# Reordering the head of a two-layer decoder trunk: row factor, head rotations, first weight load and last means

## What is computed

```
for layer in range(2):
    h = rms_norm(x, ln1_g)                  # x * rsqrt(mean(x*x) + eps) * g
    P = h @ w_in                            # 2124 columns: heads of three groups
    a = dsa_mixer(...)                      # indexer scores, top 64 keys, 4 heads, partial rotary
    b = s5_mixer(...)                       # complex diagonal state space, 16 groups of 16
    c = nsa_mixer(...)                      # compressed, selected and window branches, 8 heads
    x = x + concat(rms_norm(a), rms_norm(b), rms_norm(c)) @ w_out
    x = x + square(relu(rms_norm(x, ln2_g) @ w_up)) @ w_down
return rms_norm(x, final_g)
```

## Time and profile before

| | |
|---|---|
| time before, median of 3 runs | 732.26 us (732.01 to 736.17) |
| the profiled execution's own time | 735.1 us |
| its span | 733.1 us |
| PE busy | 664.8 us, 91% |
| DVE busy | 450.8 us, 61% |
| ACT busy | 367.1 us, 50% |
| POOL busy | 228.2 us, 31% |
| mean granted TensorE clock | 0.967 |

### The profile page before, as it was taken

The page is one execution under the profiler, slowest core; times in us unless marked ns, Lnnn a source line. Parts: engine busy times, 40 slices in busy tenths (PEclk is TensorE's granted clock), DMA queues, the critical chain, the costliest instruction groups (busy, mean ns, idle before and its releaser), DMA issues.

```text
span 733.1 us, 11482 instructions
## 1 busy us (share of the span) xinstructions
PE 664.8 (91%) x4308; PEld 586.9 (80%) x4308; DVE 450.8 (61%) x860; ACT 367.1 (50%) x680; POOL 228.2 (31%) x379
## 2 busy tenths in 40 slices
PE   5959878779899999999999987977989999999996
PEld 4847767568798899988978886756879889999884
DVE  8675974843755559596555659584375555455553
ACT  5542755563544543445545567556354444444542
POOL 5899433441034399980000001544100000000001
PEclk9988998998999999999999999999899999999998
DMA  9485020200685555637535722020065665666541
GB/s 267 125 220 149 30 41 30 73 30 29 202 237 201 170 186 169 225 119 247 168 119 164 228 79 41 30 73 30 29 202 178 196 188 171 208 182 198 177 140 57
DMA packets 62965, 102.77 MB, mean 140 GB/s; under 512 B 20677, under 2 KB 27022, under 8 KB 62878
## 3 DMA queue, kind: packets, MB, share of 16 engines
q1 hardware_dynamic: 58862, 98.63, 44.1%
q0 software_dynamic: 592, 1.70, 0.9%
q10 hardware_dynamic: 3456, 1.70, 0.9%
HBM read 99.66 MB, written 1.31 MB: 138 GB/s over the span
## 4 chain that ended last, share of the span: by engine, by line
PE 72%; DVE 14%; ACT 6%; issue 3%; DMA 2%; POOL 1%; SPq 0%; DVEq 0%; POOLq 0%; ACTq 0%
PE pb L1542 70%; DVE w_lo L1179 5%; DMA raw<-in_w_in 2%; DVE tab_zone L1437 2%; DVE x L1109 1%; ACT w_hi L804 1%; DVE dtmp L1102 1%; ACT tab_zone L1000 1%; PE pb L1675 1%; DVE h_lo L1109 1%; ACT ptmp L1007 1%; DVE cprob L1102 1%; PE pb L1825 1%; POOL sp L584 1%; ACT tab_zone L998 1%
## 5 line engine op out<-in xcount | busy, mean ns | idle before, releaser
L1179 DVE TENSOR_TENSOR w_lo<-raw,w_hi 128x1024 fp32r<-128x1024 f32 (+2 forms) x176 | 225.3, 1298 | 157.3 <-ACT w_hi L804 157.2
L804 ACT ACTIVATE w_hi<-raw 128x1024 fp32r<-128x1024 f32 (+2 forms) x184 | 187.7, 1026 | 224.4 <-PE pb L1542 200.4
L1542 PE MATMUL pb<-h_hi,w_hi 128*128 128x256 f32 x512 | 145.2, 284 | 2.5 <-DVE h_lo L1109 1.8
L1542 PE MATMUL pb<-h_hi,w_lo 128*128 128x256 f32 x512 | 144.9, 283 | 0.0
L1542 PE MATMUL pb<-h_lo,w_hi 128*128 128x256 f32 x512 | 144.9, 283 | 0.0
L1542 PEld LDWEIGHTS pb<-h_hi,w_hi 128*128 128x128 f32 x512 | 98.2, 192 | 4.1 <-DVE w_lo L1179 3.0
L1542 PE MATMUL pb<-w_hi,z_hi 128*128 128x512 f32 x256 | 99.9, 390 | 0.4 <-DVE w_lo L1179 0.4
L1542 PE MATMUL pb<-w_hi,z_lo 128*128 128x512 f32 x256 | 99.8, 390 | 0.0
L1542 PE MATMUL pb<-w_lo,z_hi 128*128 128x512 f32 x256 | 99.6, 389 | 0.0
L1542 PEld LDWEIGHTS pb<-h_hi,w_lo 128*128 128x128 f32 x512 | 98.2, 192 | 0.4
L1542 PE MATMUL pb<-w_hi,h_hi 128*128 128x512 f32 (+2 forms) x224 | 85.8, 383 | 13.9 <-DVE w_lo L1179 10.8
(11 more groups left out here) (304 smaller groups left out, 982.4 us busy)
## 6 DMA issues: line engine op xcount, KB each, us to landing
raw<-in_w_up SPq DMA_DIRECT2D x64, 512.0 KB, 3.7
raw<-in_w_down SPq DMA_DIRECT2D x64, 512.0 KB, 4.3
raw<-in_w_in SPq DMA_DIRECT2D x24, 512.0 KB, 4.7
raw<-in_w_out SPq DMA_DIRECT2D x16, 512.0 KB, 3.8
raw<-in_w_in SPq DMA_DIRECT2D x8, 308.0 KB, 3.5
raw<-in_w_in SPq DMA_DIRECT2D x8, 280.0 KB, 3.3
x<-in_x ACTq DMA_DIRECT2D x4, 256.0 KB, 4.2
u_zone<-proj SPq DMA_DIRECT2D x16, 32.0 KB, 2.1
```

Source lines behind the costliest of these rows:

```text
L804: hi_made.by(act.activation(w_hi[:, n % RING, 0:width(n)], raw[:, n % RING, 0:width(n)], ACT.Copy))
L1179: lo_made.by(dve.tensor_tensor(w_lo[:, n % RING, 0:width(n)], raw[:, n % RING, 0:width(n)], w_hi[:, n % RING, 0:width(n)].bitcast(F32), AL ...
L1542: return pe.matmul(o, l, r, start=start, stop=stop, skip_group_check=True)
```

## The change

Four edits:

1. In layer 0 POOL makes the row factor inside `prep(0)`, behind the operation on S(15) and ahead of the wait for B and the S5 input products. ACT makes its sums of squares in layer 0 right behind the sines, ahead of `hi(4)`; in layer 1 they stay where they were.
2. In both layers DVE makes `lo(12)` to `lo(15)` ahead of the heads of tile 1, which are now turned behind `lo(15)`, the sixteenth low part, and ahead of `lo(16)`.
3. SP issues the first weight piece ahead of the positions, the step row and the parameter rows; pieces 1 to 3 stay behind them.
4. At the end ACT scales by 1024^-0.5 before it squares, so that its sums are already parts of the mean; DVE adds the two and eps in one operation inside `scaled(t)`, and POOL only raises to -0.5.

```diff
+            first_pieces(0, range(1), lambda q: None)
             sp.dma_start(pos_i[:], positions...)
...
-            first_pieces(0, lambda q: None)
+            first_pieces(0, range(1, RING), lambda q: None)
...
                 tt(S(15), S(15), S(10), ALU.mult)
+                if occ == 0:
+                    rstd(0, 1, r1[:], stat[:, 0:2], D_MODEL)
                 pool.wait_ge(*s5_loaded(occ))
...
             prep(0)
-            rstd(0, 1, r1[:], stat[:, 0:2], D_MODEL)
             prep_inputs(0)
...
             for t in range(TT):
-                pool.wait_ge(tail_sq.sem, 2 * t + 2)
-                mean = tail[:, 4 + t:5 + t]
-                tt(mean, tail[:, 2 * t:2 * t + 1], tail[:, 2 * t + 1:2 * t + 2], ALU.add)
-                ts(mean, mean, 1.0 / D_MODEL, EPS, ALU.mult, ALU.add)
-                pool.tensor_tensor(r1[:, t:t + 1], mean, half_neg[:, 0:1], ALU.pow).then_inc(tail_r.sem, 1)
+                pool.wait_ge(tail_mean.sem, t + 1)
+                pool.tensor_tensor(r1[:, t:t + 1], tail[:, 4 + t:5 + t], half_neg[:, 0:1], ALU.pow).then_inc(tail_r.sem, 1)
...
                     act.activation(ang[:], ang3[:], ACT.Sin).then_inc(trig_rope.sem, 1)
+                    sums(0, 0, sq_sum.by)
                 for n in range(4, 6):
                     hi(L, n)
-                sums(L, 0, sq_sum.by)
+                if L:
+                    sums(L, 0, sq_sum.by)
...
-                                   accum_out=tail[:, 2 * t + half:2 * t + half + 1]).then_inc(tail_sq.sem, 1)
+                                   scale=D_MODEL ** -0.5, accum_out=tail[:, 2 * t + half:2 * t + half + 1]).then_inc(tail_sq.sem, 1)
...
+                for n in range(12, 16):
+                    lo(n)
                 dve.wait_ge(tile_sb.sem, tile_sb.at(L, 2))
                 step(dve.tensor_copy(iqr[:], proj[:, :, O_IQ:O_IQ + PART]))
...
                 dve.wait_ge(roped.sem, roped.at(L, 2))
-                for n in range(12, 20):
+                for n in range(16, 20):
                     lo(n)
...
             def scaled(t):
 
+                dve.wait_ge(tail_sq.sem, 2 * t + 2)
+                stt(tail[:, 4 + t:5 + t], tail[:, 2 * t:2 * t + 1], EPS, tail[:, 2 * t + 1:2 * t + 2], ALU.add, ALU.add)\
+                    .then_inc(tail_mean.sem, 1)
                 dve.wait_ge(tail_r.sem, t + 1)
```

More of the change, by code:

```diff
@@ L396, in trunk @@
         tail_sq = sig("tail_sq", 0)
+        tail_mean = sig("tail_mean", 0)
         tail_r = sig("tail_r", 0)
@@ L469, in _, with first_pieces @@
         def _(sp):
+            def first_pieces(lyr, qs, before):
+                c0, w = TILES[0]
+                for q in qs:
+                    before(q)
+                    raw_in[q].by(sp.dma_start(raw[:, q, 0:2 * w].rearrange("p (k n) -> p k n", k=2),
+                                              w_in[lyr].rearrange("(k p) n -> p k n", p=PART)
+                                              [:, 2 * q:2 * q + 2, c0:c0 + w]), 16)
+            first_pieces(0, range(1), lambda q: None)
             sp.dma_start(pos_i[:], positions.rearrange("o (t p) -> p (o t)", p=PART)).then_inc(pos_loaded.sem, 16)
@@ L560, in _ @@
                 if L < DEPTH - 1:
-                    first_pieces(L + 1, lambda q: sp.wait_ge(lo_made.sem, lo_made.at(L, PIECES + q + 1 - RING)))
+                    first_pieces(L + 1, range(RING), lambda q: sp.wait_ge(lo_made.sem, lo_made.at(L, PIECES + q + 1 - RING)))
             for t in range(TT):
```

## The result

The changed kernel is slower: 736.52 us (median of 16 runs) beside 732.31 for the kernel before, ratio 1.0049, 95% interval 1.0033 to 1.0065. That is 3.6 us (2.4 to 4.8) by the ratio, while the two medians lie 4.2 apart; by either, the time is outside the forecast range of 727.0 to 734.5, though still only half a per cent. Its profiled execution has a span of 734.8 us.

What follows compares the result with a forecast made beforehand. Layer 0 was taken as bound by DVE's work behind POOL's tables. Gains 1.5 (layer 0), 0.35 (layer 1) and 0.15 (tail), less 1.3 for late rows, gave 0.7: 731.5 us against the 732.26 median, range 727.0 to 734.5.

Steps and rivals of the forecast that it cites:

- 15.9 us of DVE's work behind the end of POOL's tables: Layer 0, from DVE coming free at 80.85 to the first attention unit at 96.73; claimed to bound that stretch, not PE.
- Every sign in layer 0 that the prediction named for being right: PE idle under 1 us before tile 3, new wait before tile 4, `ca` ending 81 to 83, first unit near 96, others.
- none for being wrong: First unit before 92 or after 99, first low part before 10, or POOL's `ca` ending well before 80.
- rival (a): DVE and POOL turns don't bind, so PE's early-tile gain reaches the units: 11 us, 721.5; chance 0.07.
- (c): Start of layer 0: rows wait behind the whole first piece (3.0), key rotations miss their gap: 733.3 to 735.5; chance 0.2.
- D = 1.3: Delay of step row, positions and parameter rows behind the first piece; bounds 0.5 and 3.0, layer 0 loses 1.3.
- The S5 products themselves end where they did, so POOL's later work isn't moved: Layer 0, row factor moved ahead of the S5 products: these still end at 30.1, tile 0's copy starts 2.6 earlier.
- PE's new wait ahead of tile 4: Layer 0: PE finishes `s5_inputs` at 58.9 and waits 3.2 for low part 16, which follows the heads.
- a forecast of 1.5: Layer 0, DVE work done before POOL's `ca` operations end: gain 1.5, with bounds 0 and 4.0.
- the first two of `s5_states`: DVE operations in layer 0 that might pass beside POOL's by the skill's rule; the sum left them behind POOL.
- 0.35 forecast: Layer 1, PE's wait of 0.33 ahead of tile 3 goes: gain 0.35 with a faster first matmul.
- 0.15 forecast: Last means at the end: second half saves 0.35, the update waits 0.2 for the first half's scaling; gain 0.15.

Runs made afterwards that it cites:

- the runs with one and two pieces ahead: Kernel before with only the first weight piece, or the first two, issued on SP's queue ahead of the rows: ratios 1.0043 and 1.0090.
- rows first: Changed kernel with the first weight piece put back behind the step row, positions and parameter rows: ratio 1.0013 to the kernel before.
- the run with four fillers: Changed kernel plus four 128x384 PE products that compute nothing, in layer 0 ahead of the wait for `cx`: ratio 1.0034 to the kernel before.
- without and with filler: Changed kernel with the first piece back behind the rows, without or with eight idle PE products ahead of the `cx` wait: ratios 1.0013 and 0.9948.
- the profile at 0.83: First run of the changed kernel with eight idle PE products in layer 0 ahead of the `cx` wait: ratio 1.0007, granted clock 0.83 throughout.

## Why the prediction was wrong

**The step that failed: the first unit taken for the end of layer 0's front.** The prediction says "what ends last ahead of the units is not PE but 15.9 us of DVE's work behind the end of POOL's tables", and sums up at the first unit at L1437. As far as that unit the total was right (forecast near 96, measured 96.29), and that is luck: edits 1 and 2 brought some 2.8 there instead of 1.5, the late rows cost some 2.3 instead of 1.3, and the two misses offset. Every sign in layer 0 that the prediction named for being right came, and none for being wrong, because all of them lie at or ahead of that unit. But the chain of the kernel before doesn't go through that unit. It goes from DVE's `cx` into the 64 small products and, after them, into the products that the next units wait for (96.07 3.92 above, then 101.77 0.29 DVE at L1437). I had followed PE's gains in the early tiles, said that they mostly go into a new wait, and put no price on waiting itself: PE's lead ahead of `cx` became 3.50 us of idle time, and the products behind it cost 2.82 more at 1.2 GHz. The price was in my own text: rival (a) counts 1.3 for matmuls that run slower behind the idle stretch ahead of tile 3. I took it as a gain when that stretch goes, and didn't ask what a new stretch would cost. None of my rivals held this; (c) found the sign and the late rows, and for the rest named a lost round of DVE and POOL, which the runs don't show. The trace of before could have warned: there PE is idle for 3.05 us before the indexer's products at 83.56, and the window 84 to 88 has a granted clock of 0.64.

**Edit 3, D = 1.3: mis-sized.** It is 3.1 at the step row, 2.3 at POOL's chain and 2.9 at the first unit when the edit stands alone, so rival (c)'s 3.0. I had both bounds and took a value near the lower one, though the only row of a small load behind a large one spoke for the upper. The Trainium skill, in "DMA: Bandwidth & Descriptors", section "Queues, rings and completion order", has descriptors of one ring taken in order; the runs with one and two pieces ahead agree, with 3.1 and 4.5 us of delay.

**Edit 1: mis-sized, in two ways that offset.** "The S5 products themselves end where they did, so POOL's later work isn't moved" is wrong. The first table operation of POOL (38.87 in the earlier trace rows) starts, over the profiles with rows first, at 38.20 to 39.44 without edit 1 and at 37.35 to 37.53 with it (three each, the kernel before aside). In the kernel before with edits 1 and 4 POOL makes the factor at 23.33 and still starts the B products at 24.05, where it started them at 24.06: a row of 1.90 us for a 128x8 operation at 19.80 had stood in that stretch, and one such turn is lost less often. Why the turns fall out that way no run was made to show. Tile 0's copy, forecast for 27.5, stands at 26.80 there and at 29.73 in the changed kernel. The late rows don't explain that: the run with four fillers has the same code and the same late rows up to there, and its copy is at 26.80. What differs is the pace of tile 0's products, 128x512 each. From 14.91 to 20.6 us they start about 0.43 us apart in the changed kernel's profile, and from 14.80 on 0.23 apart in the other's. None of this reaches the first unit (96.29 and 95.87).

**Edit 2: right on PE and DVE, wrong in worth.** Low part 15 forecast to end at 54.4, measured 55.13. The last `tab_zone` 56.7, measured 57.4. The heads to 61.3, measured 61.07. The last `ca` near 81 to 83, measured 82.03. PE's new wait ahead of tile 4 is there, 1.51 instead of 3.2. Edits 1 and 2 bring 3.1 and 2.4 us at the first unit (rows first, without and with filler) against a forecast of 1.5, inside its bounds. But the clock took all of it away (rows first: 3.1 gained at the unit, nothing at the end of the products). That turns bind, which rival (a) denied, is shown by the run without three `ca` operations. For the first two of `s5_states` it didn't matter whether they could pass beside POOL: DVE reached them at 83.20, after POOL's end at 82.03. I had said that no row shows such an operation beside a long one of POOL. One does, further on in the trace before: the unit's operation at 126.87, which reads PSUM and the mask in SBUF, takes its usual 0.29 us in the middle of a low part of 128x1024 that POOL makes from 125.28 to 127.64. The Trainium skill's rule in "SBUF — State Buffer", section "Who interferes with whom", that a DVE instruction with at most one SBUF input, outside the modes that use both ports, doesn't contend with GpSimd, agrees with that row.

**Layer 1 and the tail.** Layer 1: 0.35 forecast, 0.59 measured at the start of tile 3. Edit 4: 0.15 forecast, 0.34 measured; the wait for the first scaling, debited with 0.2, is 0.09, and the shorter mean brings 0.43 instead of 0.35.

**The sum, redone** at the end of the 64 products: edits 1 and 2 +2.8 (the mean of 3.1 and 2.4), late rows -2.3 (from 93.65 and 94.36 to 96.29: 2.6 and 1.9), clock -2.82, so -2.3, and the trace says -2.38. That isn't yet the end of the account: the loss grows to 3.97 and shrinks to 2.30 with the clock of the next stretches, so that the sum still fits at the start of layer 1 is luck too. From 2.30 layer 1's tile 3 takes off 0.59, the rest of layer 1 adds 0.36 (no run was made to show by what), and the tail takes off 0.34: 1.73 at the last scaling (729.15 to 730.88). The medians lie 4.2 apart; the profiled execution of before lies 2.8 above its median and that of after 0.4, so 2.4 us of that difference is the choice of executions.

## What to carry to other kernels

Take the end of a stretch from the chain of waits, not from the first instruction that looks like its goal: here the unit came earlier while the products beside it ended later. When an edit lets PE run ahead into a wait, read the granted clock of what follows the new idle time, and price that work at both levels (3.92 and 6.74 to 7.04 us here); if PE has nothing useful to do there, a few idle products can pay for themselves, in a dose read from the gap. Name signs that lie behind the place where the sum ends, not only ahead of it. A small load that starts a chain doesn't go behind a large one on its queue, and a bound with a row to support it should be taken over a middle value with none.

## What the runs showed of the hardware

The same 64 products of 128x32 took 3.92 us in all seven profiles with idle time of up to 0.85 us ahead, and 6.74 to 7.04 in all six with 2.61 to 4.54; no run fell between (the profile at 0.83 is left aside). The granted clock of these stretches was 1.00 and 0.50, 2.4 and 1.2 GHz. The window with the idle time itself, 92 to 96, still reads 1.00 in the changed kernel. The length of the idle time isn't shown to be the whole of it: in the kernel before, PE is idle for 2.49 us ahead of four products at 106.83, and these still run mostly at the full clock (window 104 to 108: 0.92), while what follows doesn't (108 to 112: 0.65).

The clock of a stretch can differ between executions of the same code: tile 0's products start 0.43 us apart in the changed kernel's profile and 0.23 apart in that with four fillers, which has the same code up to there. And the windows don't show all of it, since those from 12 to 20 read 1.00 in both. So the rows have to be read beside the granted clock. The 104 products behind the first units took 4.25 us in seven profiles and 5.85 to 5.92 in six; with one profile of each kernel, it isn't shown whether that goes with the edits or with the execution.

Beside POOL's operations on 128x1024, DVE's rotations of 0.2 to 0.5 us stand in rows of about 2, and they came 5.9 us earlier at the first unit when POOL's tables ended 6.64 earlier.
